# The causal mask of attention score tiles, moved from a TensorE product to a GpSimd select by position

## The chip, the cores and the metric

The kernel runs on one core of a Trainium2 chip. The metric is the time on the device of one execution, in microseconds (us). A core has TensorE (PE in the profile, its weight loads PEld), VectorE (DVE), ScalarE (ACT), GpSimd (POOL) and SyncE (SP, which here only issues DMAs). Each engine works through its own instructions in order, and waits at semaphores for the others.

## What is computed

One inference step of a small decoder: one mLSTM layer, then one multi-head latent attention layer, each followed by a gated feed-forward part with a short convolution. The prompt has 1024 positions, eight sample sequences have one each. The change lies in the prompt's attention, 16 heads over 1024 positions:

```python
MLA_HEADS = 16; QK_NOPE = 64; QK_ROPE = 32; V_HEAD = 64; SEQ = 1024
...
        sc = jnp.einsum('bqhd,bkhd->bhqk', qn, k_nope) + jnp.einsum('bqhr,bkr->bhqk', qp, kpe)
        q_pos = blk * Q_BLOCK + jnp.arange(Q_BLOCK)
        sc = jnp.where(k_pos[None, :] <= q_pos[:, None], sc.astype(jnp.float32) * ATT_SCALE, -jnp.inf)
        p = jax.nn.softmax(sc, axis=-1).astype(v.dtype)
        return jnp.einsum('bhqk,bkhd->bqhd', p, v)
```

## The kernel before

The program is a row of stages: modulation and mLSTM, the first feed-forward part, the latent, attention (about 1640 to 2195 us of the span), the samples, the second feed-forward part. In float32 every product with weights is made of three products of rounded parts, head and rest; POOL makes the two parts of each weight unit: `w_hi` (the unit times ones, rounded) and `w_lo` (the unit less `w_hi`). In attention this is `pool_split` (L1482): two instructions for a unit of 128 x 1024.

Attention takes the heads in pairs `p` of 0 to 7, head `h = 2p + e`. For a pair PE first makes the rotated parts, queries and keys (`projection`), then the row maxima of head 2p, mixed with the values (even pairs) or with output products of finished heads (odd pairs). Then come the scores of head 2p, then those of head 2p+1.

The scores of one head are eight tiles, j = 0 to 7. Tile j holds keys 128 j to 128 j + 127 in the partitions and queries from 128 j on in the columns, so it is 1024 - 128 j wide, and only its first 128 columns, the diagonal block, need a mask. Per tile:

- `scores(h, j)` on PE (L1760): three products per 512 columns (L1776), and a last one of 128 columns (L1778) that adds minus 1e30 above the diagonal, out of two constant 128 x 128 tiles.
- `exps` on ACT (L1855): the exponential out of PSUM, into `p_first` for j = 0 and into one of two `p_later` buffers for j > 0. Exponential j waits until two tiles earlier was both multiplied and added.
- `product(h, j)` on PE (L1781): probabilities times values (L1797), into PSUM. It waits for the exponential (`emptied(pe, ("scores", h, j))`).
- `add(h)` on POOL (L1527): for j = 1 to 7 the tile is added into `p_first` (L1534), out of which `sums` (L1694) makes the sums of the rows. The first add waits for product 0, since it overwrites `p_first`.

PE's order is written out by `score_fills` (L109): scores 0, scores 1, product 0, scores 2, product 1, and so on; with the even head the maxima of the next head lie between them, and a transpose `turn` (L1758) after product 6, out of which DVE makes eight rows of the next head's `q_head` (L1983), which its scores need. With the odd head `sums` of the even head stands ahead of product 0. Scores, maxima and the rest share a ring of three PSUM slots. POOL's order in a pair is, for an even pair: adds of head 2p, split of ("heads", p+1), adds of head 2p+1. For an odd pair: split of ("out", i, 0), adds of head 2p, split of ("heads", p+1) but in the last pair, adds of head 2p+1, split of ("out", i, 1).

Of the kernel before, what the change touches and what calls it, by code (L numbers as in the profile page):

```python
# [16 lines left out]
ALU = mybir.AluOpType  # L17
# [3 lines left out]
P = 128  # L21
D = 1024
KT = D // P
# [7 lines left out]
NCK = SEQ // P  # L31
# [21 lines left out]
U_PAIR = U_DQ + 3  # L53
# [38 lines left out]
UNIT_AT = {name: k for k, name in enumerate(SPLIT_UNITS)}  # L92
# [82 lines left out]
def program(nc, t, ctx):  # L175
    def sem(name):
        return ctx.enter_context(nc.semaphore(name))
# [36 lines left out]
    raw = [R(f"w_raw{j}", [P, KT, P]) for j in range(2)]  # L214
    hi = [R(f"w_hi{j}", [P, KT, P], F32R) for j in range(2)]
    lo = [R(f"w_lo{j}", [P, KT, P], F32R) for j in range(2)]
# [22 lines left out]
    dm, p_ = R("decay", [P, NCK, P]), R("p_m", [P, SEQ])  # L239
# [122 lines left out]
    N = dict(qsn=qsn, qsp=qsp)  # L362
# [120 lines left out]
    ring_full = sem("ring_full")  # L483
# [12 lines left out]
    smp_dve = sem("smp_dve")  # L496
    pv_done = sem("pv_done")
    p_added = sem("p_added")
    o_free = sem("o_free")
    at_head = sem("at_head")  # L500
    at_rest = sem("at_rest")
# [941 lines left out]
    def ring_slot(step, n=SEQ, off=0):  # L1443

        o = 1024 * (AT[step] % 3) + off
        return psf[:, o:o + n]
# [7 lines left out]
    def filled(eng, step):  # L1454

        eng.wait_ge(ring_full, AT[step] + 1)

    def emptied(eng, step):

        eng.wait_ge(ring_free[AT[step] % 3], AT[step] // 3 + 1)  # L1460

    def later(h, j):

        return 7 * h + j - 1

    def probabilities(N, h, j):

        return N["p0"][h % 2][:, :] if j == 0 else N["pr"][later(h, j) % 2][:, 0:SEQ - j * P]

    def unit_slot(name):  # L1470

        return name[2] + 1 if name[0] == "out" else 0

    def unit_rows(name, tile):

        return tile[:, 0:2, :] if name[0] == "values" else tile[:, :, :]

    def split_rows(name, tile):

        return tile[:, name[2]:4:2, :] if name[0] == "values" else tile[:, :, :]  # L1480

    def pool_split(name, after):  # L1482

        pool, u, s = nc.gpsimd, U_PAIR + UNIT_AT[name], unit_slot(name)
        h_, l_, r_ = split_rows(name, hi[s]), split_rows(name, lo[s]), unit_rows(name, raw[u % 2])
        n = 2 if name[0] == "values" else KT
        pool.wait_ge(w_loaded[u % 2], (u // 2 + 1) * 16)
        if after is not None:
            filled(pool, after)
        pool.tensor_tensor(h_, r_, ones[:, :].unsqueeze(1).to_broadcast([P, n, P]), ALU.mult).then_inc(w_head, 1)  # L1490
        pool.wait_ge(w_head, u + 1)
        pool.tensor_tensor(l_, r_, h_.bitcast(F32), ALU.subtract).then_inc(w_split, 1)

    def split_done(eng, name):
        eng.wait_ge(w_split, U_PAIR + UNIT_AT[name] + 1)

    def pool_attention(L, N):
        pool = nc.gpsimd
        fl(pool, T_DQ + 2)
        pool_split(("heads", 0), None)  # L1500
        pool.wait_ge(lat_split, 2)
        pool.wait_ge(out_done, 16 * 6)
        cos = L["cos"]
        split_done(pool, ("heads", 0))

        def one(tile, r):
            n = r.stop - r.start
            v = ones[r, :].unsqueeze(1).to_broadcast([n, NCK, P])
            pool.tensor_tensor(tile[r, :].rearrange("p (t q) -> p t q", q=P), v, v, ALU.mult).then_inc(rows_set, 1)

        def zero(tile, r):
            pool.tensor_tensor(tile[r, :], cos[r, 0:SEQ], cos[r, 0:SEQ], ALU.subtract).then_inc(rows_set, 1)

        one(N["kh"][0], AUG[0])
        for k, (tile, r) in enumerate(((N["ql"][0], AUG[0]), (N["kl"][0], AUG[0]), (N["qh"][1], slice(32, 64)),
                                       (N["kh"][1], slice(32, 64)))):
            pool.wait_ge(rows_set, k + 1)
            zero(tile, r)
        pool.wait_ge(rows_set, 5)
        one(N["kh"][1], AUG[1])  # L1520
        pool.wait_ge(rows_set, 6)
        zero(N["ql"][1], slice(32, 64))
        pool.wait_ge(rows_set, 7)
        zero(N["kl"][1], slice(32, 64))
        pool.wait_ge(rows_set, 8)

        def add(h):  # L1527
            p0 = N["p0"][h % 2]
            pool.wait_ge(pv_done, 8 * h + 1)
            for j in range(1, NCK):  # L1530
                emptied(pool, ("scores", h, j))
                if j > 1:
                    pool.wait_ge(p_added, later(h, j))
                pool.tensor_tensor(p0[:, j * P:SEQ], p0[:, j * P:SEQ], probabilities(N, h, j), ALU.add)\  # L1534
                    .then_inc(p_added, 1)

        def rotated_rest(p):
            for e in range(2):
                pool.wait_ge(rot_head, 2 * p + e + 1)
                pool.tensor_tensor(N["ql"][e][ROT[e], :], N["rot"][ROT[e], 0:SEQ], N["qh"][e][ROT[e], :].bitcast(F32),  # L1540
                                   ALU.subtract).then_inc(rot_rest, 1)
                pool.wait_ge(rot_rest, 2 * p + e + 1)
            if p:
                filled(pool, ("rope", p))
                pool.tensor_tensor(N["qh"][1][AUG[1], :], ident_row(AUG[1]), ident_row(AUG[1]), ALU.subtract)\
                    .then_inc(rows_reset, 1)
                pool.wait_ge(rows_reset, p)

        for p in range(PAIRS):
            i = p // 2  # L1550
            if p % 2 == 0:
                pool.wait_ge(smp_full, p + 1)
                for which in range(2):
                    pool_split(("values", i, which), None)
                split_done(pool, ("values", i, 1))
            rotated_rest(p)
            if p % 2 == 0:
                add(2 * p)
                pool_split(("heads", p + 1), ("values", i, 3))
                add(2 * p + 1)  # L1560
                pool.wait_ge(p_added, 7 * (2 * p + 2))
            else:
                pool_split(("out", i, 0), ("out", i - 1, KT - 1) if i else None)
                add(2 * p)
                if p < PAIRS - 1:
                    pool_split(("heads", p + 1), ("keys", p))
                add(2 * p + 1)
                pool_split(("out", i, 1), ("out", i - 1, KT - 1) if i else None)
                split_done(pool, ("out", i, 1))

# [109 lines left out]
    def pe_attention(L, N):  # L1680
        pe = nc.tensor
# [78 lines left out]
        def scores(h, j):  # L1760
            step, e, p = ("scores", h, j), h % 2, h // 2
            if j == 0:
                emptied(pe, ("turn", h))
                emptied(pe, ("queries", p))
                emptied(pe, ("keys", p))
                pe.wait_ge(rot_rest, h + 1)
                if p == 0:
                    pe.wait_ge(rows_set, 3 + 5 * e)
                    pe.wait_ge(k_rot_rest, 2)
            ring_take(step)  # L1770
            q0, r, tk = j * P, ROWS[e], slice(j * P, (j + 1) * P)
            w = SEQ - q0
            for p_, (a, b) in enumerate(((kh, qh), (kh, ql), (kl, qh))):
                for c in range(0, w, 512):
                    n = min(512, w - c)
                    pe.matmul(ring_slot(step, n, c), a[e][r, tk], b[e][r, q0 + c:q0 + c + n],  # L1776
                              start=(p_ == 0), stop=(p_ == 2 and c > 0))
            pe.matmul(ring_slot(step, P), N["am_r"][:, :], N["id_r"][:, :], start=False, stop=True)\  # L1778
              .then_inc(ring_full, 1)

        def product(h, j):  # L1781
            e, p = h % 2, h // 2
            if j == 0:
                if h >= 2:
                    pe.wait_ge(o_free, h - 1)
                if e == 0:
                    pe.wait_ge(smp_act, 2 * p + 2)
                    pe.wait_ge(smp_dve, p + 1)
            if h % 4 == 0 and j % 2 == 0:
                emptied(pe, ("values", p // 2, j // 2))  # L1790
            emptied(pe, ("scores", h, j))
            tiles = probabilities(N, h, j).rearrange("p (n q) -> p n q", q=P)
            c = P * (p % 2) + 64 * e
            for half in range(2):
                t0 = j + (j + half) % 2
                if t0 < NCK:
                    mm = pe.matmul(ps[HALF[half], 6 + e, (t0 // 2) * P:512], N["v"][:, j, c:c + 64],  # L1797
                                   tiles[:, t0 - j::2, :], start=(j == 0), stop=(j == NCK - 2 + half))
            mm.then_inc(pv_done, 1)
# [795 lines left out]
```

## Time and profile before

| | us |
|---|---|
| median of three runs | 3161.19 (3160.47 to 3164.07) |
| the profiled execution | 3151.68 |
| its span, first to last instruction | 3149.6 |
| busy: PE, PEld, DVE, POOL, ACT | 2848.4, 2560.8, 1557.7, 1262.0, 602.6 |

The profiled execution was 0.3% shorter than the median. Busy is what the profiler shows of an engine's instructions; matmuls overlap in their pipeline, so that a PE row's duration is more than the time it adds to a stream. TensorE's granted clock over the whole span was 0.942 of full speed.

### The profile page before, as it was taken

The page shows a single profiled execution, that of the slowest core. Times are in us where ns is not written, and L with a number is a line of the kernel's source. Part 1 is how long each engine was busy: PE and PEld are TensorE (multiplying, and loading weights), DVE is VectorE, ACT ScalarE, POOL GpSimd, SP SyncE. Part 2 cuts the span into 40 slices and gives each one's busy share as a digit, 9 for nine tenths or more (in the row PEclk, how much of TensorE's full clock was granted, in tenths as well). Part 3 has the DMA queues.
Part 4 walks back from the last instruction along what each step waited for, and adds up shares of the span by engine and source line. Part 5 has one row for each costly group of instructions (what it writes and reads, how often), then busy time and mean ns, then how long its engine had stood idle before and what let it go on. Part 6 is the DMA issues. An engine that isn't in the chain of part 4 may idle for free.

```text
span 3149.6 us, 41701 instructions
## 1 busy us (share of the span) xinstructions
PE 2848.4 (90%) x16960; PEld 2560.8 (81%) x16960; DVE 1557.7 (49%) x2015; ACT 602.6 (19%) x769; POOL 1262.0 (40%) x567
## 2 busy tenths in 40 slices
PE   5799999889999999999768999998659999999997
PEld 3688888779999999998655666665439999999996
DVE  3532424255555555554755555655226554555554
ACT  4211111232000000001532322231213000101002
POOL 3312222243344444444335645543113445444433
PEclk9898989899999999999878999999779999999998
DMA  5332323242212222121100000001331111111111
GB/s 204 108 96 81 96 80 98 77 105 88 67 67 73 87 73 73 67 73 42 50 31 14 24 9 22 9 22 37 89 106 41 47 40 47 53 47 47 47 40 63
DMA packets 93751, 199.88 MB, mean 63 GB/s; under 512 B 25210, under 2 KB 52218, under 8 KB 92830
## 3 DMA queue, kind: packets, MB, share of 16 engines
q1 hardware_dynamic: 93330, 197.46, 19.6%
q8 instruction: 58, 0.95, 0.1%
q10 hardware_dynamic: 336, 1.25, 0.1%
q14 instruction: 27, 0.22, 0.0%
HBM read 188.07 MB, written 10.61 MB: 63 GB/s over the span
## 4 chain that ended last, share of the span: by engine, by line
PE 82%; DVE 7%; SPq 3%; ACT 3%; issue 2%; POOL 1%; DMA 1%; DVEq 0%; POOLq 0%; ACTq 0%
PE ps L631 65%; PE ps L1776 4%; PE ps L1797 3%; PE ps L590 1%; PE ps L1749 1%; SPq L2028 1%; SPq L2031 1%; PE ps L1198 1%; SPq L2029 1%; PE ps L1190 1%; PE ps L1728 1%; PE ps L1217 1%; PE ps L612 1%; PE ps L1219 1%; PE ps L1694 0%
## 5 line engine op out<-in xcount | busy, mean ns | idle before, releaser
L554 POOL TENSOR_TENSOR w_hi<-w_raw,ones 128x1024 fp32r<-128x1024 f32 x171 | 424.0, 2480 | 1416.1 <-PE ps L631 1251.3
L631 PE MATMUL ps<-hn_head_f,w_hi 128*128 128x344 f32 x2112 | 451.9, 322 | 20.5 <-DVE hn_rest_f L794 18.0
L557 POOL TENSOR_TENSOR w_lo<-w_raw,w_hi 128x1024 fp32r<-128x1024 f32 x171 | 462.2, 2703 | 13.4
L631 PE MATMUL ps<-hn_rest_f,w_hi 128*128 128x344 f32 x2112 | 449.2, 321 | 0.0
L631 PE MATMUL ps<-hn_head_f,w_lo 128*128 128x344 f32 x2112 | 447.6, 320 | 0.0
L631 PEld LDWEIGHTS ps<-hn_head_f,w_hi 128*128 128x128 f32 x2112 | 356.0, 189 | 31.9 <-issue 31.8
L631 PEld LDWEIGHTS ps<-hn_rest_f,w_hi 128*128 128x128 f32 x2112 | 357.7, 189 | 0.0
L631 PEld LDWEIGHTS ps<-hn_head_f,w_lo 128*128 128x128 f32 x2112 | 354.0, 189 | 0.0
L684 DVE SCALAR_TENSOR_TENSOR x<-ps,mod,x 128x688 f32<-128x688 f32 x208 | 194.2, 934 | 306.7 <-PE ps L631 306.7
L902 DVE TENSOR_SCALAR norm_buf_f<-a_ext,conv_w_now 128x1024 f32<-128x1024 f32 x44 | 81.7, 1857 | 310.6 <-ACT a_ext L973 302.4
L631 PE MATMUL ps<-h_head,w_hi 128*128 128x344 f32 x1056 | 225.5, 322 | 7.5 <-DVE h_rest L923 7.5
L631 PE MATMUL ps<-h_head,w_lo 128*128 128x344 f32 x1056 | 225.7, 322 | 0.0
L631 PE MATMUL ps<-h_rest,w_hi 128*128 128x344 f32 x1056 | 223.5, 320 | 0.0
L631 PEld LDWEIGHTS ps<-h_head,w_hi 128*128 128x128 f32 x1056 | 178.4, 190 | 16.5 <-issue 8.4
L1534 POOL TENSOR_TENSOR p_first<-p_first,p_later 128x896 f32<-128x896 f32 (+6 forms) x112 | 143.3, 1280 | 113.1 <-PE ps L1797 74.3
L631 PEld LDWEIGHTS ps<-h_rest,w_hi 128*128 128x128 f32 x1056 | 178.2, 190 | 0.0
L631 PEld LDWEIGHTS ps<-h_head,w_lo 128*128 128x128 f32 x1056 | 177.8, 189 | 0.0
L980 ACT ACTIVATE h_head<-h_tmp 128x1032 fp32r<-128x1032 f32 x44 | 46.9, 1066 | 586.9 <-PE ps L631 502.3
L631 PE MATMUL ps<-hn_head_m,w_hi 128*128 128x344 f32 x600 | 130.9, 327 | 11.2 <-DVE hn_rest_m L794 8.6
L1978 DVE TENSOR_REDUCE neg_max<-ps 128x1 f32<-128x1024 f32 (+7 forms) x128 | 92.2, 752 | 86.7 <-PE ps L1751 86.3
L631 PE MATMUL ps<-hn_rest_m,w_hi 128*128 128x344 f32 x600 | 127.8, 321 | 0.0
L631 PE MATMUL ps<-hn_head_m,w_lo 128*128 128x344 f32 x600 | 127.2, 320 | 0.0
(414 smaller groups left out, 4577.0 us busy)
## 6 DMA issues: line engine op xcount, KB each, us to landing
w_raw<-in_w_units SPq DMA_DIRECT2D x187, 512.0 KB, 3.5
ada_raw<-in_ada_units SPq DMA_DIRECT2D x96, 512.0 KB, 4.4
ada_raw_start<-in_ada_units SPq DMA_DIRECT2D x16, 512.0 KB, 14.6
x<-in_x SPq DMA_DIRECT2D x8, 516.0 KB, 6.7
row_bcast<-row_scratch SPq DMA_DIRECT2D x4, 1032.0 KB, 6.0
out_y<-y_tiles SPq DMA_DIRECT2D x8, 516.0 KB, 3.0
state_s<-in_state_C SPq DMA_DIRECT2D x4, 1024.0 KB, 7.9
out_C_sample<-state_s SPq DMA_DIRECT2D x4, 1024.0 KB, 10.2
```

Of the source, the lines that this page charges most:

```text
L554: pool.tensor_tensor(hi[s][:, 0:n, :], raw[u % 2][:, 0:n, :], ones[:, :].unsqueeze(1).to_broadcast([P, n, P]), ALU.mult).then_inc(w_head, 1)
L557: pool.tensor_tensor(lo[s][:, 0:n, :], raw[u % 2][:, 0:n, :], hi[s][:, 0:n, :].bitcast(F32), ALU.subtract).then_inc(w_split, 1)
L590: mm = nc.tensor.matmul(ps[q:q + 32, bank, :], sc[:, kt * NC9:kt * NC9 + 32], w[:, 4 * k:4 * k + 4, :].rearrange("p q c -> p (q c)"), star ...
L612: mm = pe.matmul(ps[:, bank, k * NC9:(k + 1) * NC9], ada_rows[g >= G_FF - 1][:, bank - 6, k * P:(k + 1) * P], sel[:, :], start=True, stop= ...
L631: mm = nc.tensor.matmul(out(c), w, v[:, a:b], start=(first and p_ == 0), stop=(last and p_ == 2))
L684: dve.scalar_tensor_tensor(x[:, m, 0:2 * CH].rearrange("p (c n) -> p c n", n=CH), v[:, 0:2, :], g, x[:, m, 0:2 * CH].rearrange("p (c n) -> ...
L902: S_dve.done(dve.tensor_scalar(cv[:, 0:SEQ], a[:, 2:2 + SEQ], w(2), w(3), ALU.mult, ALU.add))
L980: act.activation(F["hh"][:, f, :], F["htmp"][:, f, :], ACT.Copy).then_inc(hh_ready, 1)
L1534: pool.tensor_tensor(p0[:, j * P:SEQ], p0[:, j * P:SEQ], probabilities(N, h, j), ALU.add)\
L1776: pe.matmul(ring_slot(step, n, c), a[e][r, tk], b[e][r, q0 + c:q0 + c + n], start=(p_ == 0), stop=(p_ == 2 and c > 0))
L1797: mm = pe.matmul(ps[HALF[half], 6 + e, (t0 // 2) * P:512], N["v"][:, j, c:c + 64], tiles[:, t0 - j::2, :], start=(j == 0), stop=(j == NCK ...
L1978: dve.tensor_reduce(N["nm"][:, h % 2, qt:qt + 1], ring_slot(step, (qt + 1) * P), AX.X, ALU.max, negate=True).then_inc(ring_free[F % 3], 1)
```

## The change

The 128-column mask product of each score tile is gone, and the tile's last score product now signals that it is full. Instead POOL sets the elements above the diagonal of the probabilities' first 128 columns to zero, after the exponential, with one `affine_select` (`cap`) per tile, which goes by position alone. `product` on PE now waits for this select (`p_capped`) in place of the exponential, and so does the add on POOL. Further, a weight split that stood ahead of a head's adds, or between two heads', is cut into `split_head` and `split_rest`, which stand inside the head: the first after select 1, ahead of the first add, the second after select 2. The masks of the maxima (L1751) stay.

```diff
+    p_capped = sem("p_capped")
...
-    def pool_split(name, after):
+    def split_head(name, after):
...
         pool.tensor_tensor(h_, r_, ones[:, :].unsqueeze(1).to_broadcast([P, n, P]), ALU.mult).then_inc(w_head, 1)
+
+    def split_rest(name):
...
         pool.wait_ge(w_head, u + 1)
         pool.tensor_tensor(l_, r_, h_.bitcast(F32), ALU.subtract).then_inc(w_split, 1)
+
+    def pool_split(name, after):
+        split_head(name, after)
+        split_rest(name)
...
-        def add(h):
+        nothing = pool.to_reg(0.0)
+
+        def cap(h, j):
+            emptied(pool, ("scores", h, j))
+            diagonal = probabilities(N, h, j)[:, 0:P]
+            pool.affine_select(diagonal, diagonal, [[1, P]], ALU.is_ge, nothing, base=0, channel_multiplier=-1)                .then_inc(p_capped, 1)
+
+        def add(h, unit=None, after=None):
             p0 = N["p0"][h % 2]
-            pool.wait_ge(pv_done, 8 * h + 1)
+            cap(h, 0)
             for j in range(1, NCK):
-                emptied(pool, ("scores", h, j))
+                cap(h, j)
+                if j == 1:
+                    if unit is not None:
+                        split_head(unit, after)
+                    pool.wait_ge(pv_done, 8 * h + 1)
+                elif j == 2 and unit is not None:
+                    split_rest(unit)
+                pool.wait_ge(p_capped, NCK * h + j + 1)
                 if j > 1:
                     pool.wait_ge(p_added, later(h, j))
                 pool.tensor_tensor(p0[:, j * P:SEQ], p0[:, j * P:SEQ], probabilities(N, h, j), ALU.add)\
...
                 add(2 * p)
-                pool_split(("heads", p + 1), ("values", i, 3))
-                add(2 * p + 1)
+                add(2 * p + 1, ("heads", p + 1), ("values", i, 3))
...
-                pool_split(("out", i, 0), ("out", i - 1, KT - 1) if i else None)
-                add(2 * p)
+                add(2 * p, ("out", i, 0), ("out", i - 1, KT - 1) if i else None)
                 if p < PAIRS - 1:
-                    pool_split(("heads", p + 1), ("keys", p))
-                add(2 * p + 1)
+                    add(2 * p + 1, ("heads", p + 1), ("keys", p))
+                else:
+                    add(2 * p + 1)
...
-                    pe.matmul(ring_slot(step, n, c), a[e][r, tk], b[e][r, q0 + c:q0 + c + n],
-                              start=(p_ == 0), stop=(p_ == 2 and c > 0))
-            pe.matmul(ring_slot(step, P), N["am_r"][:, :], N["id_r"][:, :], start=False, stop=True)\
-              .then_inc(ring_full, 1)
+                    mm = pe.matmul(ring_slot(step, n, c), a[e][r, tk], b[e][r, q0 + c:q0 + c + n],
+                                   start=(p_ == 0), stop=(p_ == 2))
+            mm.then_inc(ring_full, 1)
...
-            emptied(pe, ("scores", h, j))
+            pe.wait_ge(p_capped, NCK * h + j + 1)
```

POOL's rows of head 1, the odd head of pair 0, before: the last add of head 0, then the split of ("heads", 1), then the adds of head 1 (`p_first_192` is its `p_first`; 193 and 194 are the two `p_later` buffers). Its other odd heads but the last read alike.

```order
L1534 TENSOR_TENSOR p_first_191<-p_first_191,p_later_193 128x128 [waits p_added,ring_free1]
L1490 TENSOR_TENSOR w_hi_52<-w_raw_50,ones 128x1024 [waits ring_full,w_loaded0]
L1492 TENSOR_TENSOR w_lo_54<-w_raw_50,w_hi_52 128x1024 [waits w_head]
L1534 TENSOR_TENSOR p_first_192<-p_first_192,p_later_194 128x896 [waits ring_free1,pv_done]
L1534 TENSOR_TENSOR p_first_192<-p_first_192,p_later_193 128x768 [waits p_added,ring_free0]
L1534 TENSOR_TENSOR p_first_192<-p_first_192,p_later_194 128x640 [waits p_added,ring_free1]
L1534 TENSOR_TENSOR p_first_192<-p_first_192,p_later_193 128x512 [waits p_added,ring_free2]
L1534 TENSOR_TENSOR p_first_192<-p_first_192,p_later_194 128x384 [waits p_added,ring_free0]
L1534 TENSOR_TENSOR p_first_192<-p_first_192,p_later_193 128x256 [waits p_added,ring_free1]
```

The same place of the changed kernel, from the head's first select to its third add:

```order
L1542 AFFINE_SELECT p_first_192<-p_first_192 128x128 [waits ring_free0]
L1542 AFFINE_SELECT p_later_194<-p_later_194 128x128 [waits ring_free1]
L1491 TENSOR_TENSOR w_hi_52<-w_raw_50,ones 128x1024 [waits ring_full,w_loaded0]
L1558 TENSOR_TENSOR p_first_192<-p_first_192,p_later_194 128x896 [waits p_capped,pv_done]
L1542 AFFINE_SELECT p_later_193<-p_later_193 128x128 [waits ring_free0]
L1498 TENSOR_TENSOR w_lo_54<-w_raw_50,w_hi_52 128x1024 [waits w_head]
L1558 TENSOR_TENSOR p_first_192<-p_first_192,p_later_193 128x768 [waits p_added,p_capped]
L1542 AFFINE_SELECT p_later_194<-p_later_194 128x128 [waits ring_free1]
L1558 TENSOR_TENSOR p_first_192<-p_first_192,p_later_194 128x640 [waits p_added,p_capped]
L1542 AFFINE_SELECT p_later_193<-p_later_193 128x128 [waits ring_free2]
L1558 TENSOR_TENSOR p_first_192<-p_first_192,p_later_193 128x512 [waits p_added,p_capped]
L1542 AFFINE_SELECT p_later_194<-p_later_194 128x128 [waits ring_free0]
```

The split's two instructions, which stood ahead of all of the head's work, now stand behind select 1 and behind select 2, and every select from the third on stands behind an add that is queued ahead of it.

PE's rows of head 1 before: product 2, scores 4, product 3.

```order
L1797 MATMUL ps<-p_later_193,v_tokens 64x384 [waits ring_free0]
L1797 MATMUL ps<-p_later_193,v_tokens 64x384
L1776 MATMUL ps<-q_head_183,k_head_187 128x512 [waits ring_free2]
L1776 MATMUL ps<-q_rest_185,k_head_187 128x512
L1776 MATMUL ps<-q_head_183,k_rest_189 128x512
L1778 MATMUL ps<-ident_r,causal_mask_r 128x128
L1797 MATMUL ps<-p_later_194,v_tokens 64x256 [waits ring_free1]
L1797 MATMUL ps<-p_later_194,v_tokens 64x384
```

The same rows of the changed kernel:

```order
L1819 MATMUL ps<-p_later_193,v_tokens 64x384 [waits p_capped]
L1819 MATMUL ps<-p_later_193,v_tokens 64x384
L1799 MATMUL ps<-q_head_183,k_head_187 128x512 [waits ring_free2]
L1799 MATMUL ps<-q_rest_185,k_head_187 128x512
L1799 MATMUL ps<-q_head_183,k_rest_189 128x512
L1819 MATMUL ps<-p_later_194,v_tokens 64x256 [waits p_capped]
L1819 MATMUL ps<-p_later_194,v_tokens 64x384
```

The mask product is gone from the scores, and products wait for `p_capped`, a semaphore of POOL, where they waited for ACT's exponential (`ring_free`).

## Rows read from the trace of the kernel before

**Rows 1.** The page: busy time of each engine, and the ending chain by engine.

```profile
PE 2848.4 (90%) x16960; PEld 2560.8 (81%) x16960; DVE 1557.7 (49%) x2015; ACT 602.6 (19%) x769; POOL 1262.0 (40%) x567
...
PE 82%; DVE 7%; SPq 3%; ACT 3%; issue 2%; POOL 1%; DMA 1%; DVEq 0%; POOLq 0%; ACTq 0%
```

**Rows 2.** Busy time by windows: the scores of head 6, then of head 7.

```profile
core 0: us, PE busy (x) PEld busy (x) DVE busy (x) ACT busy (x) POOL busy (x), PEclk, DMA share, GB/s
...
1864.60:1882.67 18.07, 17.13 (x96) 11.25 (x94) 8.30 (x11) 6.16 (x9) 14.72 (x10) 1.00 0.09 30
1882.67:1897.68 15.01, 15.01 (x79) 8.94 (x79) 7.12 (x4) 5.21 (x8) 13.49 (x9) 1.00 0.03 9
```

**Rows 3.** The ending chain in order, heads 6 and 7: start us, us, what.

```profile
1867.34 0.06 PE ps L1778
1867.40 1.01 PE ps L1797 x4
...
1881.17 0.22 PE ps L1758
1881.41 1.22 DVE q_head L1983
1882.67 1.66 PE ps L1776 x6
...
1886.73 0.86 PE ps L1797 x4
...
1891.08 0.11 PE ps L1778
...
1896.88 0.80 PE ps L1797 x6
1897.68 1.60 PE ps L631 x6
```

**Rows 4.** Groups of instructions, attention alone, shapes together.

```profile
L1534 POOL TENSOR_TENSOR p_first<-p_first,p_later 128x896 f32<-128x896 f32 (+6 forms) x112 | 143.3, 1280 | 113.1 <-PE ps L1797 74.3 <-ACT p_later L1865 32.5
...
L1778 PE MATMUL ps<-ident_r,causal_mask_r 128*128 128x128 f32 x128 | 30.3, 237 | 0.0
```

**Rows 5.** Groups of POOL's instructions in attention, by shape.

```profile
L1492 POOL TENSOR_TENSOR w_lo<-w_raw,w_hi 128x1024 fp32r<-128x1024 f32 x15 | 40.8, 2719 | 1.2
...
L1490 POOL TENSOR_TENSOR w_hi<-w_raw,ones 128x1024 fp32r<-128x1024 f32 x15 | 35.8, 2383 | 78.0 <-PE ps L631 78.0
L1534 POOL TENSOR_TENSOR p_first<-p_first,p_later 128x896 f32<-128x896 f32 x16 | 33.8, 2110 | 74.3 <-PE ps L1797 74.3
...
L1534 POOL TENSOR_TENSOR p_first<-p_first,p_later 128x256 f32<-128x256 f32 x16 | 11.6, 728 | 6.9 <-ACT p_later L1865 5.8
L1534 POOL TENSOR_TENSOR p_first<-p_first,p_later 128x128 f32<-128x128 f32 x16 | 7.3, 455 | 8.3 <-ACT p_later L1865 8.2
```

**Rows 6.** The timeline of heads 6 and 7: start us, us, engine, instruction.

```profile
1866.09 1.03 ACT L1865 ACTIVATE p_first<-ps 128x1024 f32<-128x1024 f32 x1 [30.84 <-PE ps L1778]
...
1867.27 2.38 POOL L1492 TENSOR_TENSOR w_lo<-w_raw,w_hi 128x1024 fp32r<-128x1024 f32 x1
...
1867.44 0.92 ACT L1865 ACTIVATE p_later<-ps 128x896 f32<-128x896 f32 x1 [0.32 <-PE ps L1778]
...
1885.76 0.92 ACT L1865 ACTIVATE p_later<-ps 128x896 f32<-128x896 f32 x1 [0.30 <-PE ps L1778]
...
1887.68 4.10 POOL L1534 TENSOR_TENSOR p_first<-p_first,p_later 128x896 f32<-128x896 f32 x2 [0.39 <-PE ps L1797]
...
1888.93 0.81 ACT L1865 ACTIVATE p_later<-ps 128x768 f32<-128x768 f32 x1 [2.25 <-PE ps L1778]
...
1891.12 0.87 PE L1797 MATMUL ps<-p_later,v_tokens 128*64 128x384 f32 x4
...
1892.01 5.00 POOL L1534 TENSOR_TENSOR p_first<-p_first,p_later 128x640 f32<-128x640 f32 x4 [0.22 <-ACT p_later L1865]
```

**Rows 7.** PE's timeline at two waits of like length.

```profile
1841.47 0.67 PE L1749 MATMUL ps<-k_head,q_head 96*128 96x512 f32 x2 [2.24 <-DVE x L1990]
...
1987.68 0.67 PE L1749 MATMUL ps<-k_head,q_head 96*128 96x512 f32 x2 [2.26 <-DVE x L1990]
```

**Rows 8.** Windows after those two waits; the columns are those of [rows 2].

```profile
1844.00:1846.00 2.00, 2.00 (x6) 1.59 (x5) 0.73 (x1) 0.00 (x0) 0.00 (x0) 0.50 0.00 0
...
1988.00:1990.00 2.00, 1.60 (x8) 1.20 (x7) 2.00 (x3) 0.00 (x0) 0.00 (x0) 1.00 0.00 0
```

More of the change, by code:

```diff
@@ L1480, in split_rows @@
         return tile[:, name[2]:4:2, :] if name[0] == "values" else tile[:, :, :]
-    def pool_split(name, after):
+    def split_head(name, after):
         pool, u, s = nc.gpsimd, U_PAIR + UNIT_AT[name], unit_slot(name)
-        h_, l_, r_ = split_rows(name, hi[s]), split_rows(name, lo[s]), unit_rows(name, raw[u % 2])
+        h_, r_ = split_rows(name, hi[s]), unit_rows(name, raw[u % 2])
         n = 2 if name[0] == "values" else KT
@@ L1490, in pool_split @@
         pool.tensor_tensor(h_, r_, ones[:, :].unsqueeze(1).to_broadcast([P, n, P]), ALU.mult).then_inc(w_head, 1)
+    def split_rest(name):
+        pool, u, s = nc.gpsimd, U_PAIR + UNIT_AT[name], unit_slot(name)
+        h_, l_, r_ = split_rows(name, hi[s]), split_rows(name, lo[s]), unit_rows(name, raw[u % 2])
         pool.wait_ge(w_head, u + 1)
         pool.tensor_tensor(l_, r_, h_.bitcast(F32), ALU.subtract).then_inc(w_split, 1)
+    def pool_split(name, after):
+        split_head(name, after)
+        split_rest(name)
     def split_done(eng, name):
```

## The prediction

> **What bounds the kernel now.** I read the page first: TensorE is busy 90% of the span, and the chain that ended last lies on it for 82%, POOL holding 1% of that chain [rows 1]. So a change counts by what it takes from TensorE's stream or by where it makes that stream wait. The windows of the scores of heads 6 and 7 come next [rows 2]: TensorE is busy without a gap in the odd head (15.01 of 15.01 us), nearly so in the even one, at its full granted clock. The reader is to see POOL's column beside it: 13.49 us of 15.01 are busy already. It has 1.5 us to spare there, and no one waits for it.
>
> The chain in order shows what the mask product holds of the stream [rows 3]: 0.06 or 0.11 us each, far less than its row of 237 ns [rows 4], since matmuls overlap in the pipeline. In a head five pieces are of 0.06 and two or three of 0.11, 0.58 us in sum.
>
> **The change part by part.** *Removed:* 128 products [rows 4], 0.58 us for each of 16 heads, 9.3 us. That is all it can give.
>
> *Added:* 128 selects on POOL, of 128 x 128 in place. No select stands in this trace. The nearest row is POOL's add of 128 x 128, 455 ns [rows 5]. From 128 to 896 columns the add goes from 455 to 2110 ns, 2.155 ns a column, so 0.18 us are fixed. Bounds of a select, c: below, the fixed part alone, 0.18; above, twice the add, 0.91; a gain is excluded, since an instruction is added. I take c = 0.455: one input less to read, but a position to work out and compare.
>
> The Trainium skill (GPSIMD Engine Reference, Performance versus the Vector engine) puts a two-input operation at about 2.6 cycles an element, held by the shared read port; 2.155 ns at its 1.2 GHz are 2.6 cycles, so the trace agrees. Its section Performance pitfalls for Q7 kernels gives compare-and-select loops 1.03 to 2.03 cycles; with 0.18 us fixed that would be an estimate of c = 0.29 to 0.40, and the sum below would be 48 to 57 us in place of 61.
>
> *Moved:* product j on TensorE now waits for select j, and POOL takes select j only behind add j-1 and, in eleven heads, behind the two parts of a split. Before, adds could lag by two tiles, and a split ahead of them delayed nobody: exponential 2 ends at 1889.74 and product 2 starts at 1891.12 [rows 6]. That slack of 1.4 us would take a select; it doesn't take what is queued ahead of it.
>
> I follow an odd head with a split (seven: heads 1 to 13), on the times of head 7. Exponential 1 ends at 1885.76 + 0.92 = 1886.68 [rows 6]. Select 1 ends 0.1 (signal) + c later. From there POOL never pauses until select 7: the split, 2.38 + 2.40 = 4.78 (the undisturbed `w_hi` mean and `w_lo` [rows 5, 6]); adds 1 to 6, which are a head's adds, 143.3 / 16 = 8.96, less the last, 0.46, so 8.50 [rows 4, 5]; selects 2 to 7, 6c; and the links from a select to the add that waits for it, in tiles 3 to 6. A link is 0.15: the first six adds of head 7 stand as 4.10 and 5.00 us, 9.10 against 8.50 of work, over four dependences inside those two pieces [rows 6]. Sum 4.78 + 8.50 + 0.60 + 6c = 13.88 + 6c. Is something later than POOL on the way? Exponential j+2 needs add j, but a select and an add stand between them on POOL, c + 0.15 + 0.73 at the least [rows 5], more than the short exponentials, so no. Select 7 ends at 1886.68 + 0.1 + c + 13.88 + 6c = 1900.66 + 7c. Product 7 needs 0.1 of signal and 0.4, half of the 0.80 of the last two products [rows 3]; 0.1 comes off for the mask products of the first two tiles. The head ends at 1901.06 + 7c against 1897.68 [rows 3]: 3.4 + 7c later, 6.6 us. What follows, the next pair's projections, stands behind product 7 in TensorE's order, so it shifts by as much.
>
> An even head with a split (four: 2, 6, 10, 14), on head 6: exponential 1 ends at 1868.36 [rows 6]. The next head waits for `turn`, which stands behind product 6, and for DVE's rows. So the chain goes to select 6 only: 0.1 + c + 4.78 + (8.50 - 0.73) + 3 x 0.15 + 5c = 13.1 + 6c, then 0.1 + 0.37 for product 6, 0.22 for `turn` and 1.22 + 0.05 for DVE [rows 3]: 1883.4 + 6c, 0.1 less for the masks, against 1882.67. That is 0.65 + 6c, 3.4 us. Product 7 hides beside DVE's row.
>
> An even head without one (0, 4, 8, 12): POOL keeps up. Only product 0 waits: exponential 0 ends at 1867.12 and the product started at 1867.40 in head 6 [rows 3, 6], now 0.06 sooner, and 0.1 + c doesn't fit in 0.22. It loses 0.33 and gains 0.58: -0.25 each, -1.0 in all.
>
> Head 15, odd, no split: add 1 starts when product 0 ends, 1887.6 on the times of head 7 [rows 3, 6], then 8.50 + five links 0.75 + 6c, then 0.5: later by 6c - 0.4, 2.3 us.
>
> Sum: 7 (3.4 + 7c) + 4 (0.65 + 6c) - 1.0 + (6c - 0.4) = 25.0 + 79c, with c = 0.455 **61 us**. The gain of the mask products is in this sum already.
>
> *The clock:* TensorE now pauses up to some 3 us at a time behind split and adds. Of two pauses of 2.24 and 2.26 us in this trace [rows 7], the granted clock stood at 0.50 (the lower level, 1.2 GHz) after the one and at 1.00 (2.4 GHz) after the other [rows 8]. Some 3 us at half clock lose 1.5 us; half of the eleven heads with a split would pay it: 8 us. The Trainium skill (TensorE: Matmul & The Clock Gate, Part 1) says that the clock falls after idleness and comes back under sustained work; the two rows agree in part, since equal pauses ended differently.
>
> *Off the path:* loads of weight units on SP go by finished splits and have a whole head's time; the splits' users (the next projections, outputs) come after product 7 anyway. The register for zero is set once.
>
> 61 + 8 = 69 us on the profiled execution's 3151.68 gives 3220.7; on the median of 3161.19, **3230 us**, 2.2% more.
>
> **The rivals.**
> *Faster: POOL keeps pace.* Then the mask products' 9.3 us come back less product 0's waits (5): 3157 to 3152. For it: POOL is busy 40% of the span and has long pauses between heads. Against it: it decides from the point where 3.4 + 7c falls to nothing, and even c = 0 leaves 3.4 us an odd head, 25 in all. It needs the split hidden, and the split stands between selects 1 and 3. Chance 0.04. That the slack just balances it, within 0.2% (6.3 us, about what a measurement of this kernel can tell from no change): 0.03.
>
> *Cheap select,* c = 0.18, and no fall of the clock: 25 + 14 = 39, 3200. For it: a one-input operation. Chance 0.16 for c under 0.3.
>
> *Dear select,* c = 0.91: 97 us and 8 of clock, 3266. Against it: twice an add's time for one input. The chance for c over 0.6 is 0.14, the tail beyond 0.91 included: a mechanism in which each element costs several adds' worth.
> The same page of the Trainium skill gives loops that branch on data 12 cycles an element; by that c would be an estimate of 1.46 and the sum 140 us. No run here shows it.
>
> *The clock stays low through a stalled head* until dense work follows: another 1.5 us or so in each of eleven heads, 3245 to 3250. For it: at half clock the products still hide behind POOL's 13.88 us, so nothing brings it back. Chance 0.13.
>
> **How the numbers follow.** Forecast case, c of 0.3 to 0.6 and POOL the bound in eleven heads: 0.50, its own range 3212 to 3245. With 0.13, 0.16 and 0.14 for the slower rivals, slower has 0.93; within 0.2% 0.03; faster 0.04. The range goes from the cheap end, 3200, to the dear one, 3268: what is left out, the two cases without loss and the tails beyond the ends, is some 0.2.
>
> **What would show it.** In the profile after: no L1778; POOL's busy share up by 128c, 58 us; a row of selects whose mean is c; in an odd head TensorE busy 14.4 of some 21.6 us, waiting longest for POOL's select behind `split_rest` and add 2; even heads of pairs 1, 3, 5, 7 longer by 3.4 us, those of 0, 2, 4, 6 not longer; a granted clock under 1.00 in some odd heads. The stages outside attention are unchanged. Wrong would be: selects under 0.3 or over 0.6 us (the size), odd heads that still last 15 us (the chain), or splits that don't stand on the path.

## The result, and the profile after

| | us |
|---|---|
| before, median of four runs | 3162.27 (3160.47 to 3164.07) |
| changed kernel, median of four runs | 3214.28 (3213.45 to 3215.21) |
| ratio | 1.0165, 95% interval 1.0147 to 1.0182 |
| the changed kernel's profiled execution | 3213.45, span 3211.4 |

The change costs 52 us, 1.65%. The page, in the order of [rows 1] (busy time, then the ending chain by engine and by line):

```profile
PE 2877.0 (90%) x16832; PEld 2563.8 (80%) x16832; DVE 1553.6 (48%) x2015; ACT 602.6 (19%) x769; POOL 1286.0 (40%) x695
...
PE 77%; DVE 7%; POOL 5%; issue 3%; SPq 3%; ACT 3%; DMA 1%; POOLq 0%; DVEq 0%; ACTq 0%
PE ps L632 64%; POOL p_first L1558 3%; PE ps L1799 2%; PE ps L591 1%; PE ps L1819 1%; POOL w_lo L1498 1%; SPq L2050 1%; PE ps L1199 1%; SPq L2053 1%; PE ps L1751 1%; PE ps L1772 1%; SPq L2051 1%; PE ps L1191 1%; PE ps L1218 1%; PE ps L613 1%
```

TensorE has 128 instructions less (16832 for 16960), yet its busy time rose by 28.6 us: busy time is counted at whatever clock is granted. In attention alone (1653 to 2195 us before, 1660 to 2259 after) it rose by 21.4 us, while the granted clock fell from 0.95 to 0.90; 8.7 us more lie ahead of attention. POOL went from 1% of the chain to 5%, and what it holds there are the adds and `w_lo`; the selects don't come up among the fifteen lines listed.

The lines of the selects (duration shortest, median and longest in ns, first and last start in us), and the groups of attention that answer to [rows 4, 5]:

```profile
L1542 POOL TENSOR_SCALAR_AFFINE_SELECT p_later<-p_later x112: 287/294/315, 1664.0 to 2252.4; 128x128 f32<-128x128 f32 x112
L1542 POOL TENSOR_SCALAR_AFFINE_SELECT p_first<-p_first x16: 294/294/295, 1663.0 to 2240.2; 128x128 f32<-128x128 f32 x16
```

```profile
L1491 POOL TENSOR_TENSOR w_hi<-w_raw,ones 128x1024 fp32r<-128x1024 f32 x15 | 35.6, 2374 | 0.0
L1498 POOL TENSOR_TENSOR w_lo<-w_raw,w_hi 128x1024 fp32r<-128x1024 f32 x15 | 35.6, 2371 | 0.3
L1558 POOL TENSOR_TENSOR p_first<-p_first,p_later 128x896 f32<-128x896 f32 x16 | 33.7, 2103 | 2.0 <-PE ps L1819 2.0
```

A select takes 0.294 us, not 0.455. The adds and `w_hi` are as long as before. `w_lo` has a mean of 2371 ns for 2719: before, six of its 15 instructions took 3.23 us, each of them running beside DVE's `att_rest`, and the other nine 2.34 to 2.39; now none runs beside `att_rest`, and all take 2.34 to 2.40. POOL's busy time rose by 24.0 us, where the selects alone are 37.7: the `w_lo` of attention give back 5.2 and those of other stages 3.4, and successive POOL rows that don't wait for each other overlap by 0.04 us, which busy time counts once.

Head 7 and the 12 us of projections behind it, in windows as in [rows 2]:

```profile
1913.58:1934.93 21.35, 17.94 (x71) 9.11 (x71) 5.93 (x4) 5.21 (x8) 15.89 (x18) 0.79 0.02 7
1934.93:1947.00 12.07, 12.07 (x45) 8.11 (x44) 7.12 (x5) 0.08 (x1) 4.49 (x2) 0.80 0.04 11
```

It lasts 21.35 us in place of 15.01, and the granted clock is 0.79 over the head and 0.80 behind it, where it was 1.00. The ending chain through it, in order of time (start, us, what), shows POOL's queue as the prediction laid it out:

```profile
1917.50 0.28 POOL p_later L1542
...
1920.09 2.10 POOL p_first L1558
1922.19 0.05 POOL p_later L1542
1922.24 0.17 issue
1922.40 2.37 POOL w_lo L1498
1924.77 1.76 POOL p_first L1558
1926.53 0.26 POOL p_later L1542
1926.78 0.07 issue
1926.86 1.54 POOL p_first L1558
...
1929.99 0.21 issue
...
1931.61 0.48 issue
...
1933.23 0.64 issue
```

A link from a select to the add that waits for it is 0.07, not 0.15. Select 2, for which `w_lo` doesn't wait, delays it by 0.05 and 0.17. Toward the end POOL itself waits for exponentials, 0.21, 0.48 and 0.64 us, 1.3 in all. The timeline and 2-us windows show why:

```profile
1926.83 1.55 PE L1819 MATMUL ps<-p_later,v_tokens 128*64 128x256 f32 x4 [2.58 <-POOL p_later L1542]
1928.31 0.69 PE L1799 MATMUL ps<-q_head,k_head 128*128 128x384 f32 x1
...
1933.44 1.49 PE L1819 MATMUL ps<-p_later,v_tokens 128*64 128x128 f32 x6
```

```profile
1923.00:1925.00 2.00, 1.25 (x7) 0.48 (x3) 0.00 (x0) 0.01 (x1) 2.00 (x2) 1.00 0.00 0
1925.00:1927.00 2.00, 0.17 (x2) 0.18 (x4) 0.00 (x0) 0.36 (x1) 1.92 (x3) 0.77 0.20 66
1927.00:1929.00 2.00, 2.00 (x6) 0.82 (x7) 0.00 (x0) 0.24 (x1) 1.92 (x3) 0.50 0.00 0
...
1937.00:1939.00 2.00, 2.00 (x6) 0.37 (x5) 0.00 (x0) 0.00 (x0) 1.92 (x2) 0.50 0.00 0
1939.00:1941.00 2.00, 2.00 (x8) 1.16 (x7) 1.25 (x1) 0.00 (x0) 0.50 (x1) 0.81 0.13 36
```

Product 3 waits 2.58 us for select 3, which stands behind add 1, select 2, `w_lo` and add 2. In that wait the clock falls from 1.00 to 0.50 (2.4 to 1.2 GHz) and stays there for 13.7 us: the 12 from 1927 to 1939 and, by their means, 0.9 of the window ahead and 0.8 of the one behind. At half speed TensorE's scores come later than POOL's queue would take them. The same wait of 2.58 us stands in all seven odd heads with a split. Heads 1, 7 and 11, with a granted clock of 0.79 or 0.80, are 6.3 us longer than before; heads 3, 9 and 13, at 0.91, are 4.8 longer, and head 5, at 0.88, 5.3.

**What the profiled executions differ in besides.** The two differ by 61.8 us, the medians by 52. Attention isn't all of it: the last dense piece ahead of attention, the same instructions in both, begins 7.1 us later. Chain in order, of the kernel before and of the changed one:

```profile
1557.11 35.84 PE ps L631 x216
```

```profile
1564.17 35.88 PE ps L632 x216
```

In the first 100 us already the granted clock was 0.95 in the one and 0.86 in the other, in code that the change doesn't touch. Over all its executions the kernel before ran from 3149.34 to 3167.39 us. So I compare heads within attention, and whole times by medians.

### The profile page after: what moved, and what is told of

Same layout as the page of the kernel before. It is cut to its first block, busy times and chain, and to the rows that moved or that the text cites. A ratio compares the mean times of both kernels' runs of the same rounds, so it can differ in the third digit from the quotient of the medians.

```text
span 3211.4 us, 41583 instructions
## 1 busy us (share of the span) xinstructions
PE 2877.0 (90%) x16832; PEld 2563.8 (80%) x16832; DVE 1553.6 (48%) x2015; ACT 602.6 (19%) x769; POOL 1286.0 (40%) x695
## 4 chain that ended last, share of the span: by engine, by line
PE 77%; DVE 7%; POOL 5%; issue 3%; SPq 3%; ACT 3%; DMA 1%; POOLq 0%; DVEq 0%; ACTq 0%
PE ps L632 64%; POOL p_first L1558 3%; PE ps L1799 2%; PE ps L591 1%; PE ps L1819 1%; POOL w_lo L1498 1%; SPq L2050 1%; PE ps L1199 1%; SPq L2053 1%; PE ps L1751 1%; PE ps L1772 1%; SPq L2051 1%; PE ps L1191 1%; PE ps L1218 1%; PE ps L613 1%
## 5 line engine op out<-in xcount | busy, mean ns | idle before, releaser
L632 PEld LDWEIGHTS ps<-hn_head_f,w_hi 128*128 128x128 f32 x2112 | 355.8, 189 | 33.8 <-issue 33.6
```

What stands on the lines that cost most here:

```text
L632: mm = nc.tensor.matmul(out(c), w, v[:, a:b], start=(first and p_ == 0), stop=(last and p_ == 2))
```

## The experiments

Each kernel was timed against the kernel before on the same chip. The table is read off the timelines: how much longer than in the kernel before the heads are in sum (an even head from its first score product to that of the next head, an odd one to the end of its last product), and what the projections and maxima between pairs add.

| | seven odd heads with a split | 2, 6, 10, 14 | 0, 4, 8, 12 | 15 | heads | between pairs | whole time, medians |
|---|---|---|---|---|---|---|---|
| changed kernel | +38.7 | +9.8 | -1.2 | +0.7 | +48.0 | +9.0 | +52.0 |
| splits in parts, no selects | +20.7 | +4.1 | 0.0 | 0.0 | +24.8 | +6.4 | +31.4 |
| selects, splits as before | +16.2 | +13.8 | -1.5 | +0.7 | +29.2 | +0.6 | +29.4 |
| no mask at all | -4.4 | -2.6 | -3.3 | -0.6 | -10.9 | -0.7 | -11.3 |
| selects twice | +52.9 | +19.1 | +0.5 | +4.2 | +76.7 | +11.1 | +83.3 |
| selects aside | +29.2 | +6.4 | -3.3 | +1.3 | +33.6 | +9.5 | +54.3 |
| splits outside | +10.7 | -1.0 | -1.6 | +2.4 | +10.5 | +1.9 | +22.1 |
| selects in even heads | 0.0 | -1.8 | -1.6 | 0.0 | -3.4 | -0.2 | -3.4 |
| changed, TensorE filled | +32.0 | +8.2 | -1.2 | +0.7 | +39.7 | +3.0 | +36.3 |
| changed, once more | +36.5 | +9.8 | -1.2 | +0.7 | +45.8 | +11.3 | +53.4 |

The theory was that of the prediction: on POOL, whatever is queued between a tile's exponential and its select or add comes late, and TensorE waits. The rival: each product pays for its own select, signal and 0.3 us, wherever the rest stands.

**Splits in parts, no selects.**

```diff
 # in the kernel before; mask products and waits for the exponential stay
             for j in range(1, NCK):
                 emptied(pool, ("scores", h, j))
+                if j == 1:
+                    if unit is not None:
+                        split_head(unit, after)
+                    pool.wait_ge(pv_done, 8 * h + 1)
+                elif j == 2 and unit is not None:
+                    split_rest(unit)
```

> The kernel before with the splits alone moved into the heads in two parts, behind the exponentials of tiles 1 and 2; mask products stay, no selects. Theory 1 (POOL's queue inside a head: whatever is queued between a tile's exponential and its add or select comes late, and TensorE waits): adds may lag by two tiles, so this costs less than the whole change but not nothing. On the times of head 7, add 2 ends near 1895.5, exponential 4 waits for it, and an odd head with a split lasts 2 to 2.8 us longer, seven times; even heads not longer: 3175 to 3182 where before has 3162, plus 14 to 20 us. Theory 2 (the price is each select's own delay, signal and select, in front of each product): no selects, so no change, within 0.2%.

Ratio 1.0107, 1.0087 to 1.0127: 31 us, more than either theory said, and with no select in it. The rival can't be the whole cause. An odd head is 3.0 us longer for the 2 to 2.8 expected, and the even heads with a split, which were expected to stay as they were, are 1.0 longer each. Its head 7 (ACT, then PE):

```profile
1917.69 0.60 ACT L1878 ACTIVATE p_later<-ps 128x512 f32<-128x512 f32 x1 [3.40 <-POOL p_first L1548]
1918.34 0.65 PE L1810 MATMUL ps<-p_later,v_tokens 128*64 128x256 f32 x4 [1.54 <-ACT p_later L1878]
```

Exponential 4 waits 3.40 us for add 2, and product 4 for the exponential: adds can be late by two tiles, and two split parts are more than that. The rest of the 31, 6.4 us, stands between pairs. Part of it all is the clock's: heads 1, 3, 7 and 11, at 0.89 to 0.93, are 3.0 to 3.2 us longer, heads 5, 9 and 13, at 1.00, are 2.7 longer.

**Selects, splits as before.** The other half alone: the changed kernel with `pool_split` back at its old places.

```diff
-                add(2 * p + 1, ("heads", p + 1), ("values", i, 3))
+                pool_split(("heads", p + 1), ("values", i, 3))
+                add(2 * p + 1)
...
-                add(2 * p, ("out", i, 0), ("out", i - 1, KT - 1) if i else None)
+                pool_split(("out", i, 0), ("out", i - 1, KT - 1) if i else None)
+                add(2 * p)
                 if p < PAIRS - 1:
-                    add(2 * p + 1, ("heads", p + 1), ("keys", p))
-                else:
-                    add(2 * p + 1)
+                    pool_split(("heads", p + 1), ("keys", p))
+                add(2 * p + 1)
```

> The changed kernel with its selects, but each split whole and at its old place ahead of a head's adds. Theory 1: the split of an odd head starts in the pause between heads, 4 us ahead of select 0, so that only what is left of it delays the head: 1.4 to 2 us later than before in seven odd heads instead of 5.5; the three even heads 6, 10, 14 some 1.9 later, the others 0.3 shorter, head 15 0.7 longer: plus 15 to 20 us on before, 3177 to 3183, so 30 us faster than the whole change. Theory 2: the same number of selects in front of the same products: as the whole change, plus 50 us.

Ratio 1.0099, 1.0076 to 1.0122: 29 us, 23 less than the whole change, and 9 more than the upper end of what was expected. So at their old places the splits save 19 of the 48 us in the heads. Odd heads are 2.3 longer (1.4 to 2 expected) for 5.5 in the changed kernel. Furthest off were heads 6, 10 and 14, at 3.6, 5.0 and 5.0 for the 1.9 expected. Head 10:

```profile
2039.46 1.97 PE L1820 MATMUL ps<-p_first,v_tokens 128*64 128x512 f32 x4 [2.81 <-POOL p_first L1542]
```

```profile
2038.00:2042.00 4.00, 2.54 (x6) 0.86 (x7) 0.00 (x0) 0.00 (x0) 2.04 (x4) 0.64 0.38 129
```

The whole split stands ahead of select 0 there. Product 0 waits 2.81 us and then takes 1.97 us for 1.08: the clock again.

**No mask at all.**

```diff
-            pe.matmul(ring_slot(step, P), N["am_r"][:, :], N["id_r"][:, :], start=False, stop=True)\
-              .then_inc(ring_full, 1)
+            mm.then_inc(ring_full, 1)
```

> The kernel before with the mask products of the score tiles left out and nothing in their place (the probabilities above the diagonal are not masked): what the removal alone can give. Both theories, from the chain's pieces: 0.58 us for each of 16 heads, minus 9.3 us, 3153. If mask products held TensorE for their whole row of 237 ns it would be minus 30 us.

Ratio 0.9961, 0.9945 to 0.9977: 11.3 us, and by the heads 10.9. A mask product is worth 0.08 us of stream in an odd head and 0.10 in an even one. The gain at stake was a fifth of the loss.

**Selects twice.**

```diff
+            pool.affine_select(diagonal, diagonal, [[1, P]], ALU.is_ge, nothing, base=0, channel_multiplier=-1)\
+                .then_inc(p_once, 1)
+            pool.wait_ge(p_once, NCK * h + j + 1)
             pool.affine_select(diagonal, diagonal, [[1, P]], ALU.is_ge, nothing, base=0, channel_multiplier=-1)
```

> The changed kernel with every select issued twice, one after the other. Theory 1: the sum 25.0 + 79c with a select of 0.294 us and another 0.294 plus a link of 0.07 per tile gives 79 x 0.36 = plus 28 us on the whole change (some 52), so plus 75 to 85 on before, near 3242; seven odd heads with a split 2.5 us longer each than in the changed kernel, even heads without a split 0.4 longer at most. Theory 2: each of 128 products later by 0.36: plus 46 on the whole change, near 3260.

Ratio 1.0268, 1.0247 to 1.0288: 83 us. The heads add 28.7 to those of the changed kernel, where 79 times 0.36 is 28.4; even heads without a split pay 0.4 each for eight selects more. So the price of a select depends on where it stands, as in the sum's 79. That the sums agree so well is in part luck: heads 9 and 13 are 2.5 longer than in the changed kernel, as expected, but the other odd heads with a split by 0.9 to 4.0, the low clock having fallen on other heads (head 3 has a mean of 0.79 there and 0.91 in the changed kernel).

**Selects aside.** POOL does the same selects, on a spare tile; TensorE doesn't wait for them.

```diff
-            diagonal = probabilities(N, h, j)[:, 0:P]
+            spare = N["amask"][:, :]
+            if NCK * h + j:
+                pool.wait_ge(p_capped, NCK * h + j)
...
-            pe.wait_ge(p_capped, NCK * h + j + 1)
+            emptied(pe, ("scores", h, j))
```

> The changed kernel with the same selects at the same places on POOL, but on a spare 128 x 128 tile, and products wait for the exponential as before (the probabilities above the diagonal are not masked). Theory 1 (POOL's queue): most of the loss stays, since the adds come as late and exponential j+2 waits for add j. An odd head with a split some 4.2 us longer than before (3.0 of split alone, less 0.6 of mask product, plus five selects with links of 0.36), seven times; the four even ones with a split 0.8 longer, the others 0.8 shorter: plus 30 in the heads, with the clock's part plus 33 to 40. Theory 2 (TensorE's own wait for each select is the price): only the mask products' gain is left, minus 11.

Ratio 1.0163, 1.0142 to 1.0184. In the heads it is near what the theory said, 33.6 for 30, with 4.2 in the mean odd head (3.8 or 3.9 in five of them, 4.1 and 5.9 in the two others) and 1.6 for the 0.8 expected in even heads with a split; 9.5 stand between pairs. The rival's minus 11 is out of reach: without any wait of TensorE for a select most of the loss is there, by way of late adds. The whole time by medians, plus 54, is outside the 33 to 40 expected, and 11 more than heads and pauses explain. In its profiled execution, at 3203.16 the fastest of the five, the first score product stands 6.9 us later than in the one of the kernel before, in untouched code. Why, no run shows, and the rest stays open too.

**Splits outside the heads.**

```diff
-    SPLIT_UNITS += [("values", _i, 0), ("values", _i, 1), ("heads", 2 * _i + 1), ("out", _i, 0)]
+    SPLIT_UNITS += [("values", _i, 0), ("values", _i, 1), ("heads", 2 * _i + 1)]
     SPLIT_UNITS += [("heads", 2 * _i + 2)] if _i < PAIRS // 2 - 1 else []
-    SPLIT_UNITS += [("out", _i, 1)]
+    SPLIT_UNITS += [("out", _i, 0), ("out", _i, 1)]
...
                 add(2 * p)
-                add(2 * p + 1, ("heads", p + 1), ("values", i, 3))
+                pool_split(("heads", p + 1), ("values", i, 3))
+                add(2 * p + 1)
...
-                add(2 * p, ("out", i, 0), ("out", i - 1, KT - 1) if i else None)
                 if p < PAIRS - 1:
-                    add(2 * p + 1, ("heads", p + 1), ("keys", p))
-                else:
-                    add(2 * p + 1)
+                    pool_split(("heads", p + 1), ("keys", p))
+                add(2 * p)
+                if p == PAIRS - 1:
+                    pool_split(("out", i, 0), ("out", i - 1, KT - 1))
+                add(2 * p + 1)
+                if p < PAIRS - 1:
+                    pool_split(("out", i, 0), ("out", i - 1, KT - 1) if i else None)
```

> The changed kernel with selects on all tiles, but no split inside a head: units for the next pair's heads are split in the pause of the maxima (odd pairs) or between two heads (even pairs), output units behind the odd head. Theory 1: only what POOL can't hold is left. Even heads 0.35 shorter each, 8 times; four odd heads of even pairs and head 15 2.4 longer, heads 3, 7, 11 0.7 longer: plus 11 on before, near 3170, and 40 faster than the whole change. Theory 2: as the whole change.

Ratio 1.0061, 1.0043 to 1.0080: 22 us. Inside the heads it came out at 10.5 where 11 was expected, and head by head as listed but for head 1 (1.5 longer for 2.4) and head 2 (0.3 longer, not shorter). So moving the splits from inside the heads to these places is worth 37 of the 48 us; against the kernel's old places, as the run above shows, it is 19. The rest of the 22 isn't in attention: its first score product stands at 1665.68 us, where in all other kernels it stands at 1653 to 1662, in untouched code. Why, no run shows.

**Selects in the even heads alone,** with the splits outside.

```diff
+    def by_select(h):
+        return h % 2 == 0
...
+            if not by_select(h):
+                mm = pe.matmul(ring_slot(step, P), N["am_r"][:, :], N["id_r"][:, :], start=False, stop=True)
             mm.then_inc(ring_full, 1)
...
+            if by_select(h):
+                pe.wait_ge(p_capped, NCK * (h // 2) + j + 1)
+            else:
+                emptied(pe, ("scores", h, j))
```

> As the one with splits outside, but selects in the eight even heads alone; odd heads keep the mask product. Theory 1: even heads 0.36 shorter each (0.82 of mask products less product 0's wait and a longer end), odd heads as before: minus 3 us on before, within 0.2%. Theory 2: selects in half of the tiles, plus 25.

Ratio 0.9989, 0.9975 to 1.0004; 3151.68 for 3155.03. The heads give 3.4 us, as expected. It is the best arrangement of the select that I ran, and can't be told from no change.

**TensorE filled.** Does the clock cost anything, where TensorE waits anyway?

```diff
+            again = 0
+            if e == 1 and h < MH - 1:
+                again = (0, 0, 0, 0, 2, 1, 1, 1)[j]
+            elif e == 0 and p % 2 == 1:
+                again = (0, 0, 0, 0, 1, 1, 0, 0)[j]
-            for p_, (a, b) in enumerate(((kh, qh), (kh, ql), (kl, qh))):
+            for p_, (a, b) in list(enumerate(((kh, qh), (kh, ql), (kl, qh)))) * (1 + again):
```

> The changed kernel in which TensorE, where it would wait for POOL, makes score tiles over again (in the seven odd heads with a split tile 4 three times and tiles 5, 6, 7 twice; in the four even heads with one tiles 4 and 5 twice): the same results, 4.4 us more of matmuls in such an odd head, all in its waits. Theory A (part of the loss is the granted clock, which falls to 0.50 in the 2.6 us wait behind the split and stays there until dense work of the next projection): all seven odd heads come down to 4.5 to 4.8 us over before (three have 6.3 in the changed kernel), and projections behind them lose their extra 2.2: 8 to 15 us faster than the changed kernel, in spite of more work. Theory B (the clock doesn't matter, POOL hides it): not faster, or up to 7 us slower by the matmuls that don't fit.

> The changed kernel once more, on the same chip as the filled one, so that the two can be compared: plus 52 us on before.

The filled kernel took 3196.72 us (ratio 1.0125, 1.0104 to 1.0147), the changed one on the same chip 3213.79 (1.0166, 1.0146 to 1.0186): 17 us less by the medians with more work, where 8 to 15 had been expected; by the table's heads and pauses it is 14. Head 7 of the filled kernel, and the 12 us behind it:

```profile
1902.07:1921.63 19.56, 17.10 (x86) 9.99 (x86) 5.94 (x4) 5.21 (x8) 15.54 (x17) 1.00 0.02 7
1921.63:1933.70 12.07, 12.07 (x61) 9.31 (x61) 9.25 (x6) 2.22 (x3) 5.03 (x4) 1.00 0.04 12
```

The clock is 1.00 in both. Six of the odd heads are 4.55 longer than before and one 4.65, where in the changed kernel they are 4.8 to 6.3. In the 12 us of projections 61 matmuls fit for 45. The changed kernel's second profile had only two heads that were 6.3 longer, 3 and 7, where the first had 1, 7 and 11: which heads the long low clock takes differs from one execution to the next.

## Why the prediction was right, point by point

**The mechanism** held. POOL's queue inside a head is what TensorE waits for, and what stands in it counts more than the select's own length. Splits in parts cost 31 us without any select. Selects cost 48 us in the heads with the splits inside and 10.5 with the splits outside. And selects that TensorE doesn't wait for leave 34. Where the longest wait would stand was forecast too, and there it stood: 2.58 us for the select behind `split_rest` and add 2.

**The select, c.** Taken 0.455 from the add of 128 x 128, measured 0.294. This is the term that was mis-sized most: 79 times 0.161 is 12.7 us of the forecast's 69. By the prediction's own words a select under 0.3 is a sign that the size is wrong, and it belongs to the rival *Cheap select*, with a chance of 0.16, and not to the forecast case of 0.3 to 0.6. The estimate from the Trainium skill's rates (GPSIMD Engine Reference, Performance pitfalls for Q7 kernels) had been 0.29 to 0.40; the trace agrees with its lower end.

**The sum.** With the measured c, 25.0 + 79c is 48.2 us, and the heads gave 48.0. By kind of head: odd with a split forecast 5.5, measured 5.5 in the mean of 4.8 to 6.3; even with one 2.4, measured 2.4 in the mean of 1.7 to 3.4; even without -0.25, measured -0.3; head 15 1.4, measured 0.7. That agreement is luck. The sum holds no loss of clock, and in the filled kernel, whose clock is 1.00 in all seven odd heads, the heads cost 39.7 us. So the chain on POOL was laid out 8.5 us too long: in an odd head 4.55 measured for 5.5. Its links of 0.15 were read between adds that wait for each other, and those have this gap; from a select to its add it is 0.07 in the chain, 0.3 us less in four links. And rows that don't wait for each other overlap by 0.04 us each, some 0.4 in the ten of such a head. In the changed kernel the clock put 8.3 us back in the heads.

**The removed products** are worth 11.3 us, forecast 9.3. The pieces of the chain, read in one pair of heads, gave 0.58 for every head; it is 0.6 in an odd head and 0.8 in an even one.

**The clock.** Forecast 8 us, half of eleven heads at 1.5. The filled kernel says 14 by its heads and pauses, against either profile of the changed kernel, and 17 by the medians; in the forecast's place, the heads, it is 6 to 8, and as much again stands between pairs, where the prediction had none. The prediction had the low clock last some 3 us, for which it showed no row; here it stood at 0.50 for 13.7 us through the head's end. That was one of its rivals, *The clock stays low*, and it came true in three of seven odd heads.

**The other rivals.** *POOL keeps pace* could have given at most the 11 us of the kernel without a mask, and POOL does keep pace in the four even heads without a split. The select is not dear. Of the signs that were named, POOL's busy time rose by 24 us and not by 58, and TensorE was busy 16.0 to 18.0 us of an odd head and not 14.4: rows at half clock are longer. That the stages outside attention stay as they were held for the code and not for the time: 7.1 us ahead of attention differ between the two profiled executions. That of the kernel before was short against its median, so the forecast is best compared by medians, 3230 against 3214.

**Added up.** 69 us were forecast. Less 12.7 for the select, less 8.5 for the chain, plus 6.3 for the clock (14.3 for 8), plus 3.0 between pairs that the filled kernel has too, is 57, as measured in attention by the profile; the medians say 52. The queue was taken half as dear again as it is, 61 for 40, and the clock at little over half of its price: the forecast is nearer to the result than its terms are, because these two errors are of opposite sign.

## What to carry to other kernels

An instruction on a slack engine costs what is queued ahead of it besides what it takes: here 0.3 us of select brought 2 to 5 us of adds and splits onto TensorE's path, because a result that had been allowed to lag became one that is waited for. Before moving work to an engine that is 40% busy, read its busy share in the stretch in which the work must be done (13.5 of 15.0 us in [rows 2]), and its order there. And a stall of TensorE is paid twice when it is long enough for the clock to fall: once as the wait and again in the dense work behind it.

## What the runs showed of the hardware

GpSimd's select by position takes 0.294 us for 128 x 128 float32 in place, 0.65 of its two-input add of the same size (0.455). In the traces of the kernel before and after, the gap between two GpSimd instructions of which the second waits for the first is 0.08 us behind a select or the first part of a split, and 0.14 behind an add; where the second doesn't wait, its row starts 0.04 us before the first one's ends.

In a wait of 2.58 us the granted clock fell to half and stayed there for 13.7 us, although from the wait's end on TensorE counted as busy for all but 0.1 us. Of seven odd heads with the same wait three had it so, the others a shorter stretch (0.88 to 0.91 over the head). Work repeated for nothing in such waits made the kernel 17 us faster by medians, 14 by the rows of attention.

Executions of the kernel before spread from 3149 to 3167 us, 0.6%. Part of the spread of the profiles goes with the granted clock of the first stages, in code that is the same in all: the four with 0.95 in the first 100 us have their first score product at 1653.0 to 1659.7 us, the seven with 0.85 to 0.91 at 1659.9 to 1665.7.
